# A block of linear attention, windowed attention and 128-slot expert mixing on one core: the expert phase written out as 128 periods, with front pieces set between single slots and the two gathers alternating in pairs

## The reference, cut to what matters

```python
def block_of_this_case(h):                    # DEPTH = 1, BATCH = 1
    proj = rms_norm(h, g_mix) @ w_in          # q k v z, beta, decay of 8 linear heads; q k v of windowed attention
    o_gdn = gated_delta_net(...)              # chunks of 64: decay matrix, unit triangular inverse, scan over a 64x64 state per head
    o_swa = sliding_window_attention(...)     # 8 query heads, 2 key heads, window 128, relative bias, sinks
    h = h + concat(o_gdn, o_swa) @ w_out
    h = h + peer_experts(rms_norm(h, g_ffn))
    gate = sigmoid(rms_norm(h, g_ple) @ ple_w_gate)
    return h + gate * (p @ ple_w_proj)

def peer_experts(xb):                         # per block of 128 tokens
    qr = xb @ w_query                         # 8 heads x 2 halves x 128
    s1, s2 = scores against 128 keys each
    v1, i1 = top_k(s1, 16); v2, i2 = top_k(s2, 16)
    sc, ci = top_k(v1 + v2 (16 x 16), 16)     # 128 (head, rank) slots per token
    eid = e1 * 128 + e2; gate = softmax(sc)
    hid = einsum('thkd,td->thk', expert_u[eid], xb)     # one gathered row of u per slot: a dot product
    act = gelu(hid) * gate
    return einsum('thk,thkd->td', act, expert_v[eid])   # one gathered row of v per slot: a weighted sum
```

## Time and profile before

| | |
|---|---|
| median of the runs | 3868.45 us |
| profiled execution, span | 4090.1 us (no other time of that execution is given) |
| mean granted TensorE clock | 0.888 of full speed |
| busy | PE 3315.7 us (81%), DVE 2191.8 (54%), POOL 2278.2 (56%), ACT 992.4 (24%) |
| DMA | 1214.00 MB, mean 297 GB/s; gathers 1073.87 MB, 71.6% of 16 engines' span |

### The profile page before, as it was taken

The page is one execution under the profiler, slowest core; times in us unless marked ns, Lnnn a source line. Parts: engine busy times, 40 slices in busy tenths (PEclk is TensorE's granted clock), DMA queues, the critical chain, the costliest instruction groups (busy, mean ns, idle before and its releaser), DMA issues.

```text
span 4090.1 us, 38210 instructions
## 1 busy us (share of the span) xinstructions
PE 3315.7 (81%) x11032; PEld 1816.9 (44%) x11032; DVE 2191.8 (54%) x4881; ACT 992.4 (24%) x2278; POOL 2278.2 (56%) x2189
## 2 busy tenths in 40 slices
PE   8997757897788787887879778877888687969999
PEld 4444535453444344443535344444545253534444
DVE  1124285567444854477456744486357644574543
ACT  2112213222222132212221222212221222213332
POOL 0000055667556775767566755676566656666764
PEclk9998778898889897898889888898899798989999
DMA  3321187899789998899889978899799979999996
GB/s 125 118 75 63 39 298 263 309 363 389 264 302 335 362 358 289 316 346 365 280 313 373 365 269 297 318 360 342 278 324 369 356 260 322 352 364 373 381 355 243
DMA packets 413927, 1214.00 MB, mean 297 GB/s; under 512 B 43680, under 2 KB 137888, under 8 KB 413600
## 3 DMA queue, kind: packets, MB, share of 16 engines
q0 software_dynamic: 294912, 1073.87, 71.6%
q1 hardware_dynamic: 118816, 137.66, 9.9%
HBM read 1190.61 MB, written 20.77 MB: 296 GB/s over the span
## 4 chain that ended last, share of the span: by engine, by line
PE 54%; DVE 14%; issue 13%; DMA 7%; POOL 5%; ACT 4%; another core or an unknown queue 2%; SPq 1%; POOLq 0%; DVEq 0%; ACTq 0%
PE expert_sum L894 28%; PE bank L894 23%; DVE u_rows L1645 5%; DMA u_rows<-in_peer_u_dram,group_ids 4%; DMA w_query<-in_peer_w_query_dram 3%; PE bank L897 3%; POOL u_rows L576 3%; POOL v_rows L576 2%; ACT weight_diagonals L610 1%; ACT L610 1%; ACT arena L610 1%; DVE arena L1420 1%; DVE arena L1552 1%; DVE arena L1537 1%
## 5 line engine op out<-in xcount | busy, mean ns | idle before, releaser
L894 PE MATMUL expert_sum<-v_rows,weight_diagonals 128*128 128x512 f32 x4096 | 1871.7, 617 | 153.0 <-ACT weight_diagonals L610 116.9
L576 POOL DMA_INDIRECT v_rows<-in_peer_v_dram,group_ids x1024 | 1191.1, 1163 | 827.7 <-PE expert_sum L894 541.8
L1645 DVE CUSTOM_DVE_ANT_0 u_rows<-u_rows,ffn_in 128x1024 f32<-128x1024 f32 x1024 | 1215.7, 1225 | 454.8 <-DMA u_rows<-in_peer_u_dram,group_ids 410.3
L894 PEld LDWEIGHTS expert_sum<-v_rows,weight_diagonals 128*128 128x128 f32 x4096 | 810.4, 200 | 1161.7 <-issue 1078.0
L576 POOL DMA_INDIRECT u_rows<-in_peer_u_dram,group_ids x1024 | 1052.3, 1028 | 416.8 <-issue 371.0
L897 PE MATMUL bank<-constants,arena 128*128 128x128 f32 x968 | 184.5, 336 | 330.2 <-DVE arena L1475 82.4
L610 ACT ACTIVATE weight_diagonals<-constants,expert_weight 128x128 f32<-128x128 f32 x1024 | 331.7, 390 | 228.5 <-PE expert_sum L894 177.4
L894 PE MATMUL bank<-w_query,arena 128*128 128x256 f32 (+1 forms) x1088 | 297.6, 436 | 87.4 <-DMA w_query<-in_peer_w_query_dram 50.6
L610 ACT ACTIVATE gelu<-hidden 128x8 f32<-128x8 f32 x128 | 26.7, 208 | 1386.1 <-DVE hidden L1645 1237.0
L897 PEld LDWEIGHTS bank<-constants,arena 128*128 128x128 f32 x968 | 139.1, 171 | 392.6 <-issue 212.2
L894 PEld LDWEIGHTS bank<-w_query,arena 128*128 128x128 f32 x1088 | 231.6, 215 | 155.7 <-issue 59.6
(11 more groups left out here) (166 smaller groups left out, 1968.1 us busy)
## 6 DMA issues: line engine op xcount, KB each, us to landing
w_query<-in_peer_w_query_dram SPq DMA_DIRECT2D x64, 1024.0 KB
u_rows<-in_peer_u_dram,group_ids POOLq DMA_INDIRECT x1024
v_rows<-in_peer_v_dram,group_ids POOLq DMA_INDIRECT x1024
w_channel<-in_w_in_dram SPq DMA_DIRECT2D x12, 512.0 KB
conv_scratch<-conv_out SPq DMA_DIRECT2D x12, 512.0 KB, 2.6
arena<-conv_scratch SPq DMA_DIRECT2D x8, 768.0 KB
tok_scratch<-token_out SPq DMA_DIRECT2D x8, 648.0 KB
arena<-tok_scratch SPq DMA_DIRECT2D x8, 648.0 KB
```

Of the source, the lines that this page charges most:

```text
L576: nc.gpsimd.indirect_dma_start(ring[:, j, :], None, table, bass.IndirectOffsetOnAxis(ids[:, half, j:j + 1], 0)).then_inc(landed[j], 16)
L894: return nc.tensor.matmul(out_, lhsT, rhs, start=start, stop=stop, **kw)
L1645: v.tensor_tensor_reduce(u_ring[:, j, :], u_ring[:, j, :], xb[:], 1.0, 0.0, ALU.mult, ALU.add, hid[:, g * G + j:g * G + j + 1]).then_inc(u ...
```

## The change

All loops over tiles of the expert phase are gone; every engine is written out as NP = 8 x 16 = 128 periods, and all semaphore targets are constants. Four things move.

1. `fill(n)` takes the next n of a group's 8 single steps (a dot on DVE, a slot on PE). Calls of `fill` stand inside the front pieces, ahead of their waits; what is left of the 8 is done at the period's end.
2. DVE computes the weights of group q-1 in period q, after two dots of group q (`begin`), and no longer at the end of group q-1. PE does the slots of group q-1 in period q.
3. POOL issues v rows of group q-1 and u rows of group q in alternating pairs.
4. The pieces are cut a little differently: `project_out(0)` and `project_out(1)` both stand in period 8 of a tile on PE, `attention_norm` moves from period 5 to 6, `piece10` from 8 to 7, `piece12` with query pair 0 from 10 to 9 on PE, `best_pair`s to periods 10 to 13, `pick` and `gates` to 13 and 14 on DVE.

```diff
-            def gather_group(t, g, half):
...
-                for table, ring, used, landed in ((table_u, u_ring, u_used, u_landed), (table_v, v_ring, v_used, v_landed)):
-                    for j in range(G):
-                        if j % 2 == 0 and not first:
-                            pool.wait_ge(used, n - G + j + 2)
...
+            for q in range(NP):
+                e, g = divmod(q, NG)
+                late = g == 0 and e > 0
+                if late:
+                    for pair in range(G // 2):
+                        gather_v(q - 1, pair)
+                if late or q == EARLY:
+                    take_ids(e)
+                nc.gpsimd.tensor_copy(ids[:, q % 4, :], eid[:, g * G:g * G + G]).then_inc(group_ids_ready, 1)
...
+                for pair in range(G // 2):
+                    if q and not late:
+                        gather_v(q - 1, pair)
+                    gather_u(q, pair)
...
             def level(t, l):                                     # PE
                 n = 10 * t + 2 * (l - 1)
+                fill(1)
                 for r in range(2):
                     pe.wait_ge(inv_ready, n + r + 1)
...
                     last.then_inc(level_x, 1)
+                fill(1)
                 for r in range(2):
                     pe.wait_ge(level_x_out, n + r + 1)
...
             def level(t, l):                                     # DVE
                 for r in range(2):
+                    fill(2 if r == 0 else 1)
                     dve.wait_ge(level_p, 10 * t + 2 * (l - 1) + r + 1)
...
+            for q in range(1, (NT - 1) * NG):                    # PE
+                slots = expert_slots(q - 1)
+                for i in front_piece(q):
+                    pieces[i](q // NG + 1)
+                fill(G)
...
+            def begin(q):                                        # DVE
+                fill(2)
+                if q:
+                    expert_weights(q - 1)
+                e, g = divmod(q, NG)
+                if e and g == 0:
+                    publish_gate(e)
+                if e and g == 1:
+                    experts_out(e - 1)
...
+            for q in range((NT - 1) * NG):
+                dots = expert_dots(q)
+                begin(q)
...
+                for i in front_piece(q):
+                    pieces[i](q // NG + 1)
+                fill(G)
+                if q % NG == NG - 1:
+                    publish(q // NG + 1)
```

298 lines of the change are left out of this document (160 added, 138 removed).

## The result

The changed kernel took 4006.39 us (median of 4 runs, 4000.71 to 4012.24), the kernel before beside it 3870.48 us (4 runs, 3862.61 to 3877.56): ratio 1.0357, 95% interval [1.0336, 1.0379]. The forecast was 3717 us with a range of 3565 to 3920.

A forecast was written before the change was run, and what follows sets the result against it. Gathers were taken as starved by PE's order of work, with 42 us of hand-overs a tile. 394 + 29 = 423 us a tile saves 160 us in seven; 4090.1 - 160 = 3930, times 0.9458, gives 3717 us, range 3565 to 3920.

The forecast's parts named there:

- The base: Whole kernel: profiled span 4090.1 us less 160 gives 3930, scaled by the runs' median share of the span, 0.9458, to 3717 us.
- the parts of the sum: One tile: the new distribution of work saves 5 us, and hand-overs between engines fall from 42 to 29 us.
- The hand-overs of before: One tile's 16 periods: 441.1 us measured against 399 if each lasted as its busiest engine or feed; 42 us between.
- Tile 423: Each of tiles 0 to 6 was to take 394 + 29 = 423 us instead of 445.9.
- the 394 of the sum: One tile's 16 new periods, each costed as the largest of feed, PE and DVE, without hand-overs: 394 us.
- the residue of 29: Hand-over time left in a tile, from slower gathers (17 us) and uncovered chain hops (12 us); bounds 0 and 42.
- rival B: Front periods: weights come late, PE waits at each period's head, so no change; about 3865 us, chance 0.11.
- First phase and last tile: Stretches outside tiles 0 to 6, left unchanged; alternating gathers worth between -10 and +10 us there.
- rival C: All periods: DVE's spread dots hold up POOL's gathers, 27.9 us a period, 466 a tile; slower, 4002 us, chance 0.17.
- rival D: POOL's order: u pairs still wait behind v pairs waiting for PE slots; half the gain lost, 3790 us, chance 0.07.
- The signs: Expected in tiles 0 to 6: 423 us each, DMA near 0.95, shorter POOL, DVE and PE waits, clock above 0.90.
- The sign of being wrong: Chain pieces, periods 5 to 8, longer than 29 + 21 + 21 + 32 us together by over 20 us.

## Why the prediction was wrong

**The base.** The step that failed most is "The runs' median is 0.9458 of the span, and I scale by it". The prediction noted that nothing else was known of the profiled execution, and treated the missing 5.4% as if it lay evenly on everything, the gain included. It did not: the tiles of the kernel before take 416.4 us each on a fast chip (2915.0 / 7), 445.9 in the earlier trace rows. The forecast of 423 us for a tile of the changed kernel was, scaled, a forecast of 400, and the "gain" of 23 us a tile was, against the right base, a loss of 7. In numbers: the scaled forecast holds 2800.9 us for tiles 0 to 6 and 916.2 for the rest. Unscaled, the former is 3121.4 - 160 = 2961.4, and the rest of before on a fast chip is 3868.3 - 2915.0 = 953.3. The scaling thus took away 160.5 and 37.1 us, 198 of the 286 us by which the span of 4002.8 lies above the forecast. The other 88 are 33 in tiles 0 to 6 and 55 in the last tile and around it. The gain had a second flaw: the parts of the sum give 5 + 13 = 18 us a tile, for a tile of 441.1 us; taking 423 from the mean of 445.9 added 4.8 us a tile, 34 in seven, that no part of the change explains.

**The hand-overs of before.** "The 42 us between are hand-overs between engines. The change attacks these 42 us, and the unevenness in the 399." In the same tile on the fast chip the 16 periods sum to 411.06 us, and by the same rule (the busiest engine or 21.1) to 377, so 34 lie between. In the changed kernel on that chip the rule gives 380 and the periods 423.00. Both parts of the argument fail: the new distribution is worth nothing (380 for 377), and the hand-overs grew, from 34 to 43 us. What the earlier trace rows showed above 411 belongs to that chip; about half of it is the scan's 41.30 for 26.55. The mark of it was on the profile: a wait ended by "remote", 50.8 us in six places, which the prediction doesn't mention.

Two periods of the changed kernel in that tile (the same columns as the earlier trace rows; 8 and 14):

```profile
1623.81:1650.88 27.07, 26.08 (x88) 12.44 (x89) 9.86 (x18) 7.17 (x16) 10.83 (x12) 1.00 0.59 225
...
1779.75:1811.59 31.84, 16.12 (x32) 6.79 (x32) 30.28 (x55) 5.53 (x13) 22.25 (x21) 0.73 0.90 331
```

Period 8, forecast as the longest with 32 us, takes 27.07 and is dense on PE; the longest is 14, forecast at 21.1, with DVE busy for 30.28 us. "The 29.17 us that DVE had in one period are now spread over two" was read off the list of pieces, where one pick stands in period 13 and one in 14. The fills undo that. In order of time on DVE:

```profile
1778.48 1.23 DVE L1691 CUSTOM_DVE_ANT_0 u_rows<-u_rows,ffn_in 128x1024 f32<-128x1024 f32 x1 [0.36 <-DMA u_rows<-in_peer_u_dram,group_ids]
...
1791.43 0.22 DVE L1643 SCALAR_TENSOR_TENSOR expert_id_new<-arena 128x64 f32<-128x64 f32 x1
1791.58 1.22 DVE L1691 CUSTOM_DVE_ANT_0 u_rows<-u_rows,ffn_in 128x1024 f32<-128x1024 f32 x1
...
1802.90 0.22 DVE L1643 SCALAR_TENSOR_TENSOR expert_id_new<-arena 128x64 f32<-128x64 f32 x1
```

The last dot of group 13 (1778.48) is filled in inside the best pair, so that its gelu goes ahead of the first pick (ends with L1643 at 1791.43); two dots of group 14 stand between the picks, and the other six behind the second pick (1802.90) and the gates. Both picks thus lie between two gelus, where the kernel before has them in two periods (13 and 15), and PE has a clock of 0.73 there, for 0.78 in the period of the picks in the earlier trace rows.

**Tile 423.** Tiles 1 to 6 took 422.6 us each in the first trace, 426.5 on chip 1. The size was right, in part by errors that cancelled: the floor came out at 380 us for the 394 of the sum (periods 5 and 8 shorter by 6 each, 9 to 12 by 10 together, 13 by 7, period 14 longer by 9), the hand-overs at 43 for the residue of 29. The residue is the term that was mis-sized: the wait for late weights stood in it at nothing.

**The weights (rival B).** "The first slot of each period needs weights computed after two dots of that period [...] covered only if PE still has slots left at the end of the period before; [...] two are left, 3.5 us", and later "leftover slots cover it in most periods". This is the mechanism that decided on a fast chip. PE waits for diagonals 73 times in the 112 periods of tiles 0 to 6 of the changed kernel (first trace), for 14 times in the kernel before on chip 1, which is the sign that the prediction gave for B. Moving the weights back takes PE's wait for them from 465.9 to 218.2 us and 13 us from each of tiles 1 to 6; B had priced it at 22 a tile (1.4 x 16). B's time, 3865, was "no change" only because it started from the wrong base. In the last tile there are no front pieces and no leftover slots at all, and ACT's gelu stands behind a product that stands behind the slots. "First phase and last tile [...] I leave as they are" missed that an order written out for 128 periods also changes the 16 that have no front: 49 us.

**The first tile.** Not in the forecast: 438.1 for 412.7 us, 8 of which are only a first gelu that comes 8 us earlier. On chip 1:

```profile
546.32:596.83 50.51, 16.58 (x32) 6.95 (x32) 46.85 (x156) 5.50 (x12) 27.89 (x28) 0.64 0.78 291
...
754.54:804.91 50.37, 37.71 (x132) 19.52 (x130) 17.15 (x31) 14.50 (x37) 26.41 (x27) 0.91 0.79 310
```

Two best pairs, a pick of four heads and the gates stand in the first (DVE busy 46.85), pieces 7 and 8 with both projections in the second (PE busy 37.71).

**The gathers (rival C)** were right to be doubted: their mean stayed at 1.12 us, far from 1.4. C's time, 4002 us, lies beside the measured 4006 by accident. By the Trainium skill (SBUF — State Buffer, section SBUF: two separate sides) gathers stall while VectorE holds the shared port. A gather beside dots does take longer, 1.99 us for 0.94; that it is the port no run shows. In total it makes no difference whether the dots come in bursts or spread: the mean of a gather is 1.11 us in the kernel before and 1.12 in the changed one, both on chip 1.

**The alternation (rival D)** was priced only together with the rest. Without it the new order costs another 27% (5083.74 for 4014.07 on chip 3), so the order does what it says; alone it gains 0.8% over the written out loops, 4 us a tile, the only part of the change that is shown to have earned something on a fast chip beside the loops' 0.3%.

**The signs.** In tiles 0 to 6 of the changed kernel: DMA 0.92 for 0.95, POOL's wait for v slots 367.4 us for "under 250", DVE's for u rows 610.7 for "under 150", PE's longest wait for weights 23.4 us for "gone". The kernel before on chip 1 has 295.2 and 336.4 us of the first two waits there, less than the changed one. Tiles near 423 (427.8), the gathers' mean and the clock (0.904) came as said, but the clock is no gain: the kernel before has 0.909 on chip 1 and the changed one 0.898. The sign of being wrong didn't show either: periods 5 to 8 take 109 us in that tile for the 103 of the sum. The loss was not in the chain.

What stays open: why two of the chips are slower, whether they always are, and how much of it the late starts behind PE's products make, whether the alternation alone gains there too, what single steps cost apart from the new cut of the pieces, and where the rest of the first tile's loss sits.

## What to carry to other kernels

If a profile's span and the runs' median differ by 5%, find out which waits make the difference before working with either; don't scale. A wait whose releaser the trace can't name, that lasts several us and always at one line, is the place to look. When a step is moved behind others "by two dots", follow the ring that it closes in the stretch that has nothing to cover it, here the last tile. And when a change has four parts, the cheap one alone (POOL's order) may be the one that pays.

## What the runs showed of the hardware

- One kernel takes 3865 to 3871 us on three chips and 4081 to 4082 on two, with intervals of a few tenths of a per cent on each. The size of the difference depends on the kernel: some 5.5% for the kernel before, 4.3% with its loops written out (3863.2 and 4030.6 us), 1.5 to 1.8% for the changed one.
- On the two, DVE starts up to 7.3 us behind the recorded end of the PE products that it waits for in the kernel before, and up to 4.0 us in the changed one; in the run without fills on one of them, and in every kernel on the three, it is at most 0.1 us in all 16 places. What it depends on is not shown.
- The mean granted clock was 0.909 in the kernel before and 0.898 in the changed one (154 and 466 us of PE's waits for weights, both on chip 1), and 0.815 with the gathers in blocks (1452 us of them, chip 3).
- A table load of ACT takes 1.28 us, and in the last tile it stands in the loop of waits.
- Loops written out gain 0.3% on one kind of chip and 1.2% on the other.
